# A two-layer decoder trunk with 64 experts: the shared expert outside the weight ring, the split of x on ScalarE, norm rows loaded last

## What is computed

```python
for i in range(DEPTH):                       # DEPTH = 2
    h = even_mixer(x, ...) if i % 2 == 0 else odd_mixer(x, ...)
    x = layer_norm(ALPHA * x + h, ln1_g[i], ln1_b[i])
    m = moe_ffn(x, router_w[i], router_bias[i], w1, w3, w2, sw1, sw3, sw2)
    x = layer_norm(ALPHA * x + m, ln2_g[i], ln2_b[i])
    x = x + sigmoid(x @ ple_w_gate[i]) * rms_norm(p[i] @ ple_w_proj[i], ple_norm_g[i])

def moe_ffn(x, ...):                         # 64 experts, 8 of them for a token
    shared = (silu(xf @ sw1) * (xf @ sw3)) @ sw2
    s = sigmoid(xf @ router_w); sb = s + router_bias
    # the best 4 of 8 groups by the sum of their two best sb, then the best 8 experts in them
    gates = sel / sum(sel) * ROUTED_SCALE
    # for each chosen expert: y = (silu(xe @ w1[e]) * (xe @ w3[e])) @ w2[e] * gate, added to its tokens
    return shared + routed
```

## Time and profile before

| what | value |
|---|---|
| median of 3 runs | 1390.09 us (1389.2 to 1393.08) |
| profiled execution, its own time | 1392.05 us |
| its span | 1390.3 us |
| PE busy | 1340.6 us, 96% |
| DVE, ACT, POOL busy | 487.0, 339.3, 100.8 us |
| moved by the DMA engines | 461.85 MB, 332 GB/s over the span |
| chain that ended last | PE 67%, DMA 22%, DVE 9% |

### The profile page before, as it was taken

One profiled execution on the slowest core, in us unless ns is written; L12 is line 12 of the kernel. 1 busy time (PEld: TensorE's weight loads), 2 busy tenths in 40 slices (PEclk: granted clock), 3 DMA queues, 4 the chain that ended last, 5 costly groups with the idle time before them and its releaser, 6 DMA issues.

```text
span 1390.3 us, 21098 instructions
## 1 busy us (share of the span) xinstructions
PE 1340.6 (96%) x8658; PEld 814.8 (59%) x8658; DVE 487.0 (35%) x805; ACT 339.3 (24%) x869; POOL 100.8 (7%) x107
## 2 busy tenths in 40 slices
PE   9989999999999999988999999999999999999898
PEld 4555765655656555554498557656565565555444
DVE  1484633232332322323501146332323323232244
ACT  1253232222222222221210222322222222222112
POOL 2442310000000000000100023000000000000000
PEclk9999999999999999999999999999999999999999
DMA  9720479999999999998654404899999999999981
GB/s 305 289 92 1 181 286 421 420 421 421 421 421 421 422 421 421 420 420 351 216 195 164 196 4 182 326 421 421 421 420 421 421 421 421 421 421 420 421 341 60
DMA packets 78230, 461.85 MB, mean 332 GB/s; under 512 B 6337, under 2 KB 6561, under 8 KB 27969
## 3 DMA queue, kind: packets, MB, share of 16 engines
q1 hardware_dynamic: 75552, 452.06, 79.8%
q0 software_dynamic: 2592, 8.53, 2.0%
HBM read 459.52 MB, written 1.05 MB: 331 GB/s over the span
## 4 chain that ended last, share of the span: by engine, by line
PE 67%; DMA 22%; DVE 9%; issue 1%; ACT 1%; DVEq 0%; SPq 0%
PE ps L1060 24%; DMA ring<-in_exp_w_dram 21%; PE ps L1085 11%; PE ps L1103 7%; PE ps L725 4%; PE ps L1215 4%; DVE o_tok L1873 3%; PE ps L829 3%; PE ps L913 3%; PE ps L937 2%; PE ps L898 1%; PE ps L745 1%; PE ps L606 1%; PE ps L656 1%; PE ps L574 1%
## 5 line engine op out<-in xcount | busy, mean ns | idle before, releaser
L1060 PE MATMUL ps<-ring,proj 128*64 128x256 f32 x2048 | 234.6, 386 | 14.9 <-DMA ring<-in_exp_w_dram 14.8
L1085 PE MATMUL ps<-ring,qkT 128*64 128x512 f32 x1024 | 233.8, 598 | 0.0
L1060 PEld LDWEIGHTS ps<-ring,proj 128*64 128x64 f32 x2048 | 149.3, 139 | 107.9 <-issue 23.2
L1873 DVE TENSOR_TENSOR o_tok<-ps,o_tok 128x1024 f32<-128x1024 f32 x124 | 151.9, 1225 | 79.9 <-PE ps L1103 78.7
L1879 DVE TENSOR_TENSOR y_lo<-ps,y_hi 128x1024 fp32r<-128x1024 f32 x62 | 76.0, 1225 | 227.5 <-ACT y_hi L1430 227.5
L1865 DVE SCALAR_TENSOR_TENSOR roped<-roped,rows,ps 128x256 f32<-128x256 f32 x64 | 30.8, 481 | 341.5 <-ACT roped L1403 326.7
L1085 PEld LDWEIGHTS ps<-ring,qkT 128*64 128x64 f32 x1024 | 67.8, 136 | 111.8 <-issue 110.4
L1060 PE MATMUL ps<-ring,pT 128*64 128x256 f32 x1024 | 121.9, 380 | 3.0 <-DMA ring<-in_exp_w_dram 3.0
L1430 ACT ACTIVATE y_hi<-ps 128x1024 fp32r<-128x1024 f32 x62 | 63.5, 1024 | 240.9 <-PE ps L1085 240.9
L1060 PE MATMUL ps<-ring,gb_row 128*64 128x256 f32 x1024 | 121.4, 379 | 0.0
L1103 PE MATMUL ps<-y_hi,selT 128*128 128x512 f32 x248 | 110.4, 445 | 10.5 <-DVE o_tok L1873 8.7
(11 more groups left out here) (276 smaller groups left out, 1446.1 us busy)
## 6 DMA issues: line engine op xcount, KB each, us to landing
ring<-in_exp_w_dram SPq DMA_DIRECT2D x180, 2048.0 KB, 20.4
ring<-in_exp_w_dram SPq DMA_DIRECT2D x24, 1024.0 KB, 7.0
ring<-in_od_w_in_dram SPq DMA_DIRECT2D x6, 2048.0 KB, 8.3
ring<-in_ple_w_gate_dram SPq DMA_DIRECT2D x4, 2048.0 KB, 12.6
ring<-in_ev_w_in_dram SPq DMA_DIRECT2D x3, 2048.0 KB, 19.3
ring<-in_sh_w_dram SPq DMA_DIRECT2D x6, 1024.0 KB, 7.8
ring<-in_ev_w_o_dram SPq DMA_DIRECT2D x2, 2048.0 KB, 10.2
ring<-in_od_w_o_dram SPq DMA_DIRECT2D x2, 2048.0 KB, 8.1
```

Source lines behind the costliest of these rows:

```text
L1060: ins = pe.matmul(ps[b * SLOTS:(b + 1) * SLOTS, 2, w * FE:(w + 1) * FE], xe(odd, c)[:, u * P + b * SLOTS:u * P + (b + 1) * SLOTS], views[b ...
L1085: ins = pe.matmul(ps[b * SLOTS:(b + 1) * SLOTS, 4 + half, :], hT[:, f, b * SLOTS:(b + 1) * SLOTS], views[b][:, f, half * PIECE:(half + 1) ...
L1873: dve.tensor_tensor(y_acc[:, t, :], ps[:, bank:bank + 2, :].rearrange("p b n -> p (b n)"), y_acc[:, t, :], ALU.add)\
```

## The change

The shared expert leaves `items`, so the experts have all four slots from the start. Its w1, w3 and w2 go to memory that attention has done with: w1 to `qkT`, w3 to `o_tok`, w2 to the upper half of `proj` (`shared_load`). To make room, `x_hi` lies in `proj` and the even octets' gathered x in `xT` and `proj`. The router and the choice of tile 0 stand ahead of the end of the output projection (`router`, `choose`). Four instructions of the choice are left out or joined. The shared expert's down and its copy stand in pairs 0 and 1 (`shared_down`, `shared_add`). ScalarE makes `x_hi`, GpSimd only the rest. The layer norm multiplies by the row while it waits for the root. The norm rows are loaded when the layer's last w2 has landed, and the last pair's w2 comes in two halves.

```diff
-        x_hi = nc.alloc_sbuf_tensor_at("x_hi", [P, NT, D], F32R, offset=xT_at)
+        x_hi = nc.alloc_sbuf_tensor_at("x_hi", [P, NT, D], F32R, offset=proj_at)
...
-            shared_item[L] = len(items)
-            items.append(("shared", ("shared_down", L, 0)))
+            expert_item[L] = len(items)
...
+            def shared_load(L):
+
+                units = FIRST_UNIT[L] + len(UNITS[L % 2])
+                sp.wait_ge(sem("sc_mm"), units)
+                sp.dma_start(shared_w1, a["sh_w1"][L].rearrange("(p c) f -> p c f", c=DC)).then_inc(sem("shared_w1_loaded"), 16)
...
+                sp.wait_ge(sem("pv_mm"), units)
+                sp.dma_start(shared_w2, a["sh_w2"][L].rearrange("(p f) n -> p f n", f=2)).then_inc(sem("shared_w2_loaded"), 16)
...
+                            for half in range(2):
+                                cols = slice(half * PIECE, (half + 1) * PIECE)
+                                for b in range(2):
+                                    w2 = ring[:, (s + b) % RING, DOWN0:DOWN0 + 2 * D].rearrange("p (c f) -> p c f", c=2)
+                                    sp.dma_start(w2[:, :, cols], a["exp_w2"][L, e + b].rearrange("(p c) f -> p c f", c=2)[:, :, cols])\
+                                      .then_inc(down_loaded[(s + half) % RING], 16)
...
                 pool.wait_ge(sem("exp_up"), L * PAIRS + PAIRS - 4)
+                last = expert_item[L] + NE - 1
+                pool.wait_ge(down_loaded[last % RING], down_loaded_at[last])
                 load_rows(L, 1)
...
-                wo(L, 1, 1, range(DC))
+                wo(L, 1, 1, range(0, 1))
+                pe.wait_ge(sem("layer_loaded"), 48 * (L + 1))
+                router(L, 0)
+                wo(L, 1, 1, range(1, DC))
...
                     exp_up(m, o, odd, u, par, first and M0 == 0)
+                    if isinstance(m, int) and m < NT:
+                        shared_down(m)
...
+                        if m == 1:
+                            pe.wait_ge(sem("shared_added"), NT * (L + 1))
...
+                def x_high(t):
+                    act.wait_ge(sem("ln1_out"), NT * L + t + 1)
+                    act.activation(x_hi[:, t, :].rearrange("p (c n) -> p c n", c=DC),
+                                   x_tok[:, t, :].rearrange("p (n c) -> p c n", c=DC), ACT.Copy).then_inc(sem("x_high"), 1)
...
                     silu(m)
+                    if isinstance(m, int) and m < NT:
+                        shared_add(m)
                     hT_copy(m)
...
+                        if which == 1 and t == 1 and half == 1:
+                            choose(L, 0)
...
-                    rsqrt(mean_var[:, 1:2], 1.0, LN_EPS)
+                    variance(mean_var[:, 1:2], 1.0, LN_EPS)
                     dve.wait_ge(sem("gb_loaded"), 32 * (j + 1))
                     seq(dve.scalar_tensor_tensor(x_tok[:, t, :], summed[:, t, :], mean_var[:, 0:1], gb_row[:, 0, :], ALU.subtract, ALU.mult))
+                    rsqrt_end()
```

More of the change, by code:

```diff
@@ L438, in _ @@
+                        with sp.Fori(1, NE // UNROLL - 1) as i:
+                            for u in range(0, UNROLL, 2):
+                                pair_load(i, u)
+                        pair_load(NE // UNROLL - 1, 0)
+                        pair_load(NE // UNROLL - 1, 2, halves=True)
                         k = e0 + NE
@@ L707, in attention, with router @@
                 transpose_tile(x_tok, 0)
-                wo(L, 1, 1, range(DC))
+                wo(L, 1, 1, range(0, 1))
+                pe.wait_ge(sem("layer_loaded"), 48 * (L + 1))
+                router(L, 0)
+                wo(L, 1, 1, range(1, DC))
+            def router(L, t):
+                wait_tile("xT", 3 * L + 1, t)
+                for c in range(DC):
+                    ins = pe.matmul(ps[:, 6 + t, 0:NE], xT[:, c, t * P:(t + 1) * P], router_w[:, c, :],
+                                    start=(c == 0), stop=(c == DC - 1))
+                ins.then_inc(sem("router_mm"), 1)
             def transpose_pairs(m):
@@ L954, in up_all, with down_all, down_tile @@
                     return ins
-                def up_tile(slot, t, between):
-                    w1, w3, _ = ffn_views(slot)
-                    for b, w in enumerate((w1, w3)):
-                        if b == 1 and t == 0:
-                            between()
+                def down_all(slot):
+                    _, _, w2 = ffn_views(slot)
+                    for t in range(NT):
+                        ins = down_tile(w2, t, 2 * t)
+                    return ins
+                def down_tile(w2, t, bank):
+                    for half in range(2):
@@ L975, in down_all, with shared_up, shared_down @@
+                    return ins
+                def shared_up(t, blocks):
+                    for n in blocks:
+                        for c in range(DC):
+                            ins = pe.matmul(ps[:, 4 + t, n * P:(n + 1) * P], (shared_w1, shared_w3)[n // 2][:, c, n % 2::2],
+                                            xT[:, c, t * P:(t + 1) * P], start=(c == 0), stop=(c == DC - 1))
                     return ins
-                def router(t, L=L):
+                def shared_down(t, L=L):
@@ L979, in router @@
                     if t == 0:
-                        pe.wait_ge(sem("layer_loaded"), 48 * (L + 1))
-                        pe.wait_ge(sem("var_ready"), 3 * NT * L + NT)
-                    for c in range(DC):
-                        ins = pe.matmul(ps[:, 6 + t, 0:NE], xT[:, c, t * P:(t + 1) * P], router_w[:, c, :],
-                                        start=(c == 0), stop=(c == DC - 1))
-                    ins.then_inc(sem("router_mm"), 1)
-                def between(L=L):
-                    router(0)
-                    pe.wait_ge(sem("ln1_out"), NT * L + 2)
-                    transpose_tile(x_tok, 1)
@@ L993, in _ @@
[L993 to L1001 removed]
+                        pe.wait_ge(sem("shared_w2_loaded"), 16 * (L + 1))
@@ L1082, in exp_down @@
                     for half in range(2):
+                        if half and by_half:
+                            k = ks + 2 + 2 * par
+                            pe.wait_ge(down_loaded[k % RING], 32 + down_loaded_at[k])
                         for f in range(2):
```

254 lines of the change are left out of this document (133 added, 121 removed).

## The result

The changed kernel takes 1376.92 us (median of 4 runs, 1375.96 to 1377.61) beside 1390.91 for the kernel before on the same chip: ratio 0.9899, 95% interval 0.9885 to 0.9913, 14.0 us less. The forecast was 1371.4, with 1365 to 1380 as range. Direction and mechanism hold; the gain forecast was 18.7 us, and 14.0 came. The profiled execution took 1377.61 us (span 1375.8), 14.4 less than that of before.

The account below looks back on a forecast made before the run. The stream of paired expert weight loads bounds the kernel, by its start plus its length. 2 x (5.0 queue + 3.2 norm rows + 0.3 second norm) + 1.7 clock = 18.7 us, so 1371.4 against the median; range 1365 to 1380.

Parts of the forecast that it names:

- The front: Router, choices and gather up to the first pair: first up starts 8.0 us earlier, at 178.8 instead of 186.84.
- The moved downs: Shared downs in pairs 0 and 1 add 2.8 and 3.4 us; second w2 load issued at 212.4.
- The queue: Start of the paired loads: second w2 lands at 219.6 instead of 224.6, everything behind 5.0 us earlier.
- the first gap: Start of the paired loads: first of two gaps forecast in the DMA share, near 196; the second near 213.
- "After that ... no more gap": Stream behind the second w2: TensorE's pair of 14.3 us against the queue's 14.9 lets no more gap open.
- The norm rows: Layer end: rows moved behind weights save 3.2 us (2.5 to 4.1), landing at T + 13 (T: last w3 landed).
- The clock (1.7): Layer 0's last up takes 3.67 us instead of 5.36, shorter waits without the rows: 1.7 us once.
- The second norm (0.3): Second norm of each layer: its earlier product with the row gives 0.3 us a layer.
- the halves (nothing): Last pair's w2 loaded by halves, ahead of the last down: gives nothing.
- norm rows late: Second norm: rows landing at T + 19.0 make it wait 3.3 us a layer; 1378.0 us, chance 0.17.
- Slower: Layer end: norm rows starve behind SyncE's queue, each layer waits 12 us; 1395.4 us, chance 0.05.
- TensorE the bound: Expert pairs: TensorE becomes the bound, so the change doesn't shorten the stream; 1385.9 us, chance 0.05.

Follow-up runs that it names:

- the doubled subtraction: Changed kernel with GpSimd making each subtraction that gives x_lo twice; ratio 0.9970 to the kernel before.
- both downs ahead: Changed kernel with both shared-expert downs and ScalarE's copies moved from pairs 0 and 1 to behind the fourth gather, ahead of the first pair; ratio 0.9945.
- downs spread: Changed kernel with the shared downs in the scatters of pairs 8 and 12, adding in PSUM, shared w2 in free memory, ScalarE's two copies gone; ratio 0.9842.
- the one with the rows early: Changed kernel with GpSimd loading the two norm rows once the fourth pair from the end is up, not behind the last w2; ratio 0.9932.
- spread in 22 and 26: Kernel with shared downs in the scatters of pairs 8 and 12, with them in those of pairs 22 and 26 instead; ratio 0.9851.
- in 1 and 2: Kernel with shared downs in the scatters of pairs 8 and 12, with them in those of pairs 1 and 2 instead; ratio 0.9876.
- with earlier rows: Kernel with shared downs in the scatters of pairs 8 and 12, norm rows fetched after the first half of the last w2; 1369.29 us, ratio 0.9844.

## Why the prediction was right, and where its size was off

- **The front: right.** 8.0 forecast, 8.2 net measured in either layer. One duration in it was wrong without harm: ScalarE's copy of x takes 2.10 us, not 1.03 (the row I took it from reads PSUM), but TensorE's shared block lies beside it. That the choice costs 4.8 without GpSimd was right (5.0 and 4.8), and the reason is now shown by the doubled subtraction: VectorE was held by GpSimd, though at 162.89 by a subtraction and not by a cast.
- **The moved downs: right.** The second w2 was to be issued at 212.4; it was at 212.45 net.
- **The queue: this is the step that failed in its size.** "The second w2 goes out at 212.4 and lands at 219.6" took 7.2 us for a 2 MB load, from 4.7 for 1 MB plus 2.5 of transfer. It took 9.2; the first w1 took 8.1 and the first w2 9.4. The 6.8 given beside it in the prediction was further off. Two loads of 1 MB do come in 7.3 into the empty queue; one of 2 MB took 8.1, and at the drained places the second MB came 3.8 behind the first. Most of the miss is ahead of the second w2: the first w2 landed at 204.0 net instead of 201.8, so the first gap lost 3.2 us instead of 1.9, and the w3 before the second w2 was already 2.0 late. The second gap lost 2.8, as forecast. In layer 0 3.0 us net were gained instead of 5.0. In layer 1 the second w2 landed 12.7 us earlier, of which 8.3 are layer 0's: 4.4.
- **"After that ... no more gap": wrong in layer 1.** The w1 issued at 899.65 landed 5.9 us behind its predecessor and the w3 issued at 902.95 6.4, so 2.3 us were lost behind the second gap. The w3 had been issued 6.7 us ahead, so TensorE's pace did not cause its 1.4; the cause is open.
- **The norm rows: right in kind, large in size.** 3.2 forecast; the stretch from the second w2 to the last w3 got 2.9 us shorter in layer 0 (419.6 to 416.6) and 1.4 in layer 1, from which the 2.3 above have been taken. Undone, they cost 2.6 in the stream. The upper bound of 4.1 had a misreading in it: of the earlier trace rows 2.6 are the rows (28.61 against 26.05), and the 1.5 in the last stretch (27.60) are the late load that the kernel with both downs ahead shows without any rows. They landed at T + 14.6, not T + 13. The rival *norm rows late* needed 1.3 us more than that.
- **The clock (1.7): the number right, by luck.** 1.7 came, but the reason given, that without the rows the waits are shorter, is not borne out: two kernels without the rows there (downs ahead, downs spread) had the slow last up again, and the one with the rows early did not.
- **The second norm (0.3) and the halves (nothing): right**, with 0.4 and no difference.
- **The sum.** 3.0 + 4.4 for the streams' starts, 2.9 + 1.4 for the rows, 1.7 and 0.7 make 14.1. Layer 1's unchanged attention gave 1.6 more and the offset of layer 0 took 1.3: 14.4, as the two profiled executions differ. Of the 4.6 us that were missing against 18.7 in these terms, 2.6 are the landing, 2.1 the rows' term with the losses behind the second gap.
- **The rivals.** *Slower* by starving rows did not come: they passed SyncE's queue in 8 us. *TensorE the bound* fell too: layer 0's last w3 followed the landing of the second w2, 1.5 and 1.5 us later with both downs ahead, 5.8 and 5.5 earlier with them spread. But TensorE does bound the start of the stream. I counted the 4.8 us lost at the gaps as the price of an early start; they were the price of the two downs' place, and the spread kernel took them back.
- **Not taken apart.** No run puts the shared expert back into the ring. Before, the fourth expert's 3 MB went out at 182.49, ahead of the first paired load; now they go out at 157.65 and have landed by 167.3. What this alone is worth, and the router's earlier place or the four instructions left out, is not shown.

## What to carry to other kernels

When a queue of loads is the bound, keep it from draining: put extra work of the releasing engine where the queue is deep, not in the first iterations, and look for sums in PSUM that can take it in without an eviction of its own. Work on GpSimd that nobody waits for can still hold short VectorE instructions on the path, to the end of its own; place it in time, whichever engine prepares for it. Take a duration only from a row with the same source memory, order of columns and size: the copy and the 2 MB load were both taken from a neighbour, and came out a half and a fifth too cheap.

## What was unexpected of the hardware

- A 0.20 us VectorE instruction was held 3.33 us, through a GpSimd subtraction and the memset behind it, and ended 0.05 us after the latter, while one of two inputs was held 1.70 us and released between two casts. 5.7 us of GpSimd's work a layer cost 9.9 us in all.
- ScalarE's copy of 128x1024 from SBUF with the columns taken in another order took 2.10 us, and GpSimd's cast of the same 2.02. ScalarE's copy of 128x1024 from PSUM, in plain order, took 1.03. Which of the two differences costs it is not shown.
- A 2 MB load into an empty queue took 8.1 us (7.9 to 8.9 at the same place of layer 0 in eight other kernels), one issued 1.2 to 1.4 us before the queue drained 9.2 to 9.4, and it landed 7.8 to 8.2 behind its predecessor, against 5.0 in a full queue. As two loads of 1 MB: 4.8 for the first, 8.2 to 8.3 for the second; into the empty queue 4.7 and 6.9.
- With some 20 us of loads queued, single 2 MB loads landed 6.1 to 6.4 us behind the previous one instead of 5.0; the cause is open.
- TensorE's clock after an idle time. Ahead of the place counts, 3.3 us of idle went with a granted clock of 0.51 from 176 to 183, and a block of 16 matmuls took 3.73 us instead of 2.10. Ahead of the last up of layer 0, the rows of eight kernels sort by that idle time: with 2.47 (before), 2.52 (downs ahead) and 2.53 (spread in 8 and 12) the last up takes 5.36 us; with 1.23 to 1.28 (changed kernel, rows early) and 2.10, 2.17 and 2.25 (spread in 22 and 26, in 1 and 2, and with earlier rows) it takes 3.67. The rows of three of these (the first 14 or 16 of the up's 32 matmuls):

```profile
639.59 1.73 PE L1090 MATMUL ps<-ring,xT 128*64 128x256 f32 x14 [1.28 <-DMA ring<-in_exp_w_dram]
```

```profile
633.72 1.95 PE L1082 MATMUL ps<-ring,xT 128*64 128x256 f32 x16 [2.25 <-DMA ring<-in_exp_w_dram]
```

```profile
634.13 2.18 PE L1082 MATMUL ps<-ring,xT 128*64 128x256 f32 x14 [2.53 <-DMA ring<-in_exp_w_dram]
```

The first is the changed kernel's, the second that of the kernel with spread downs and earlier rows, the third that of the one with spread downs alone; in brackets the idle time. But idle time alone does not decide. Two ups of the kernel before, layers 0 and 1, behind the same 2.12 us:

```profile
597.92 3.67 PE L1060 MATMUL ps<-ring,proj 128*64 128x256 f32 x32 [2.12 <-DMA ring<-in_exp_w_dram]
```

```profile
1289.65 5.36 PE L1060 MATMUL ps<-ring,proj 128*64 128x256 f32 x32 [2.12 <-DMA ring<-in_exp_w_dram]
```

The second ran at a granted clock of 0.76 over 1289 to 1296, the first at 1.00. With both downs ahead, an up of layer 1 behind 2.39 us took 3.67. What else decides is open; where it falls, it cost 1.7 us.
